# A two-layer hybrid decoder trunk: GpSimd makes the low part of the weights in steps of 128 columns in place of 256

## The reference

```python
for l in range(DEPTH):                                   # DEPTH = 2
    h = rmsnorm(x, norm_g[l]) * (1.0 + scale) + shift    # scale, shift, gate from silu(c) @ w_mod[l]
    parts = split_cols(h @ w_in[l])                      # 1024 x 8224
    y_a = hgrn2_mixer(...) * silu(a_g)                   # 4 heads, gated recurrence
    y_b = mla_mixer(...) * silu(b_g)                     # 8 heads, latent attention
    y_c = retention_mixer(...) * silu(c_g)               # 4 heads
    merged = (sigmoid(m_a) * (y_a @ w_pa[l]) + sigmoid(m_b) * (y_b @ w_pb[l])
              + sigmoid(m_c) * (y_c @ w_pc[l]))
    x = x + gate * (merged @ w_out[l])
return rmsnorm(x, final_g)
```

## Time and profile before

| | before |
|---|---|
| median of 3 runs | 1389.4 us |
| the profiled execution | 1386.04 us |
| its span | 1384.2 us |
| TensorE busy, mean granted clock | 1306.4 us, 94%; 0.986 |
| VectorE busy | 724.0 us, 52% |
| ScalarE busy | 639.5 us, 46% |
| GpSimd busy | 590.7 us, 43% |
| GpSimd, L643, `w_lo` | 736 pieces of 128x256, mean 822 ns, 579.7 us |
| TensorE in the chain of waits | 80% of the span |
| VectorE in the chain of waits | 13% |
| GpSimd in the chain of waits | 0% |

### The profile page before, as it was taken

How to read it: one execution, slowest core, us unless ns; L and a number is a source line. 1 busy time by engine, 2 the same in 40 slices (tenths; PEclk the granted TensorE clock), 3 DMA queues, 4 the chain that set the end, 5 groups by cost and what they waited for, 6 DMA issues and landing times.

```text
span 1384.2 us, 16588 instructions
## 1 busy us (share of the span) xinstructions
PE 1306.4 (94%) x5920; PEld 1036.3 (75%) x5920; DVE 724.0 (52%) x1163; ACT 639.5 (46%) x987; POOL 590.7 (43%) x751
## 2 busy tenths in 40 slices
PE   3999889999999999999979988999999999999996
PEld 2877777787777777788858777778777777778884
DVE  6778786534654434353356777662345431433333
ACT  3365545544554343444335555554355434435431
POOL 3254334654323445455526334445532253454551
PEclk9999999999999999999989999999999999999998
DMA  9322111443222323242212211123312222222221
GB/s 363 121 77 63 60 62 63 142 136 102 77 78 101 126 84 116 98 134 95 94 68 92 77 61 62 65 72 122 107 54 69 77 92 84 91 84 93 98 92 61
DMA packets 40786, 131.84 MB, mean 95 GB/s; under 512 B 5248, under 2 KB 5376, under 8 KB 39424
## 3 DMA queue, kind: packets, MB, share of 16 engines
q1 hardware_dynamic: 30336, 111.57, 23.5%
q10 hardware_dynamic: 10368, 19.21, 4.6%
HBM read 128.13 MB, written 2.10 MB: 94 GB/s over the span
## 4 chain that ended last, share of the span: by engine, by line
PE 80%; DVE 13%; ACT 4%; issue 2%; DMA 1%; POOL 0%; DVEq 0%; ACTq 0%
PE ps_st L760 20%; PE ps_st L762 20%; PE ps_st L761 20%; PE ps_o L782 5%; PE ps_s L811 2%; PE ps_s L856 2%; PE ps_s L880 1%; PE ps_w L865 1%; DVE hg_at L1434 1%; DVE hg_e L1367 1%; PE ps_misc L777 1%; DVE cq_raw L1604 1%; DVE hg_e L1366 1%; PE ps_w L726 1%; PE ps_misc L768 1%
## 5 line engine op out<-in xcount | busy, mean ns | idle before, releaser
L643 POOL TENSOR_TENSOR w_lo<-raw,w_hi 128x256 fp32r<-128x256 f32 x736 | 579.7, 822 | 752.6 <-ACT w_hi L934 752.6
L760 PE MATMUL ps_st<-h_hi,w_hi 128*128 128x512 f32 x984 | 400.3, 407 | 1.0 <-DVE merged L1303 1.0
L762 PE MATMUL ps_st<-h_hi,w_lo 128*128 128x512 f32 x984 | 383.9, 390 | 0.0
L761 PE MATMUL ps_st<-h_lo,w_hi 128*128 128x512 f32 x984 | 383.3, 390 | 0.0
L760 PEld LDWEIGHTS ps_st<-h_hi,w_hi 128*128 128x128 f32 x984 | 184.8, 188 | 45.8 <-issue 7.4
L761 PEld LDWEIGHTS ps_st<-h_lo,w_hi 128*128 128x128 f32 x984 | 185.0, 188 | 42.0 <-issue 6.2
L762 PEld LDWEIGHTS ps_st<-h_hi,w_lo 128*128 128x128 f32 x984 | 184.7, 188 | 39.6
L934 ACT ACTIVATE w_hi<-raw 128x1024 fp32r<-128x1024 f32 x184 | 193.2, 1051 | 26.6 <-PE ps_st L762 23.5
L956 ACT ACTIVATE gate_t<-gate_x 128x512 f32<-128x512 f32 x80 | 50.4, 630 | 230.5 <-DVE gate_x L1252 230.3
L1252 DVE TENSOR_SCALAR gate_x<-ps_st 128x512 f32<-128x512 f32 x79 | 54.4, 689 | 192.0 <-PE ps_st L762 191.8
L958 ACT ACTIVATE gate_t<-gate_t,cs 128x512 f32<-128x512 f32 x80 | 57.9, 724 | 2.6
(11 more groups left out here) (280 smaller groups left out, 2014.5 us busy)
## 6 DMA issues: line engine op xcount, KB each, us to landing
raw<-w_stream SPq DMA_DIRECT2D x184, 512.0 KB, 3.4
mod_w<-w_mod ACTq DMA_DIRECT2D x64, 256.0 KB, 2.7
pro_w<-w_mod_first SPq DMA_DIRECT2D x8, 1024.0 KB, 14.0
x<-x_t SPq DMA_DIRECT2D x4, 512.0 KB, 7.5
ret_decay<-decay ACTq DMA_DIRECT2D x2, 1024.0 KB, 6.3
out_t<-o_t SPq DMA_DIRECT2D x8, 256.0 KB, 2.1
raw_extra<-w_stream SPq DMA_DIRECT2D x2, 512.0 KB, 20.0
cs<-cst SPq DMA_DIRECT2D x1, 836.0 KB, 7.8
```

The lines of the kernel that those rows point to most:

```text
L643: ins = nc.gpsimd.tensor_tensor(lo[:, r], whole[:, r], hi[:, r].bitcast(F32), ALU.subtract)
L760: nc.tensor.matmul(dst[0:m, :], wh, hi, start=(k == 0), stop=False)
L761: nc.tensor.matmul(dst[0:m, :], wh, lo, start=False, stop=False)
L762: last = nc.tensor.matmul(dst[0:m, :], wl, hi, start=False, stop=(k == nk - 1))
```

## The change

GpSimd's loop steps over the columns of an item by `P` = 128 in place of `2 * P` = 256. The data, the arithmetic, and the waits and signals at a burst's ends stay as they are.

```diff
                     pool.wait_ge(w_hi_ready, e.at(w_hi_ready, i + 1))
-                    for a in range(0, n, 2 * P):
-                        r = slice(a, a + 2 * P)
+                    for a in range(0, n, P):
+                        r = slice(a, a + P)
                         ins = nc.gpsimd.tensor_tensor(lo[:, r], whole[:, r], hi[:, r].bitcast(F32), ALU.subtract)
                     ins.then_inc(w_lo_ready, 1)
```

## The result

The changed kernel takes 1370.59 us (median of 4 runs, 1366.31 to 1372.43) against 1388.86 us (median of 4, 1388.32 to 1389.75): 18.3 us faster by the medians. The ratio of the two is given as 0.985, with a 95% interval of 0.983 to 0.988, which is 20.7 us. The forecast was 10.8 us faster, with a range of 1369 to 1389. The direction was right, and the gain was forecast at little more than half of its size.

The account below looks back on a forecast made before the run. The prediction took TensorE as the bound, busy 1306.4 of 1384.2 us. Its terms, -8.0 - 2.0 - 0.8 - 3.0 + 3.0 = -10.8 us, took the median 1389.4 to 1378.6, range 1369 to 1389.

Parts of the forecast that it names:

- Whether the engines disturb each other, and how: GpSimd pieces and VectorE operations reading SBUF take strict turns; each contended operation would wait 0.29 us instead of 0.55.
- term B: TensorE's waits for hg_x: both waits at 84.76 to 88.16 go, three others shorten; -2.0 us, bounds 0 and -3.7.
- The new piece: GpSimd's 128-column piece lasts 0.49 us instead of 0.75, from a slope of 2.02 ns a column.
- Term A: TensorE's waits for hg_kd in the heads: contended VectorE operations ahead wait less; -8.0 us, bounds 0 and -11.
- Term C: TensorE's wait for h_lo at 716.6: three contended operations save 0.26 us each; -0.8 us, bounds 0 and -1.6.
- Term E: Longer GpSimd bursts make low parts late at four places (74.22, 262.48, 730.55, 931.56); +3.0 us, bounds 0 and +11.
- Term D: TensorE's clock falls after four hg_kd waits of 3.73 to 3.76 us; shorter waits save 3 us, bounds 0 and -6.8.
- Rival 1: Another wait stands right behind the shortened one and the clock still falls: -2.8 us, 1386.6 us; chance 0.17.
- Rival 2: VectorE's loss is conserved: twice the pieces, each blocking half as long; only the +3.0 us cost remains, 1392.4; chance 0.10.
- Rival 3: A GpSimd piece is nearly all fixed cost, so new pieces block like old ones: 1408 us; chance 0.03.
- Rival 4: More than forecast: all clock drops go and the hg_kd gain reaches -11: -20 us, 1370 us; chance 0.08.

Follow-up runs that it names:

- e3_fill128: The changed kernel with one extra float32 matmul ahead of TensorE's wait for hg_kd in heads 1 and 2 of each layer: 1364.61 us, 0.982.
- e2_hold256: The kernel before, 256-column pieces, with GpSimd holding back eight bursts a layer until VectorE has passed: 1361.11 us, 0.981.

## Why the prediction was right in direction and too small

**Whether the engines disturb each other, and how:** right for hg_e. It takes strict turns with the pieces, and the loss per turn halves with the piece: 0.27 us where 0.29 was forecast. It is not a rule for all of VectorE: L1413 loses less than a turn, and under term B stands an operation that got no turn for five us.

**The new piece:** 0.467 us against 0.49, a burst of eight undisturbed 3.42 against 3.59. The second size came from an addition in the prologue, and its slope of 2.02 ns was a little low.

**Term A, hg_kd, -8.0: this is the step that failed.** It measured -13.1: 1.55 us in head 0, 1.86 in heads 1 and 2 and 1.28 in head 3, where 0.9, 1.2 and 0.67 stood. hg_e and hg_q were counted nearly rightly (in heads 1 and 2 the four hg_e save 1.17, not 1.04). What the sum had wrong lies behind them. It had hg_qc's two scalings (L1413, L1415) at nothing, without a reason, and gave hg_kd 0.15. The three save 0.27 us each, 0.81 a head, of which L1411's new loss takes back 0.10 to 0.31; the sum had that loss for head 0 only, at 0.29. Heads 1 and 2 thus save 0.69 behind hg_e, where 0.15 stood. Over the eight heads this makes some 4.5 of the missing 5.1 us, and hg_e and hg_q most of the rest. The reason for the slip is visible in the rows above: for the two scalings every instance of before is disturbed, their minimum is 628 and 711 ns, and an even duration looks undisturbed. The shapes should have warned: 128 columns at 0.64 us beside a 256-column subtraction at 0.41.

**Term B, hg_x, -2.0:** -1.0. The two waits at 86 and 88 went, as forecast, but a new one of 0.9 us came at 741.59 in the second layer. Behind it stands a copy on VectorE (L1290), the first row of before, the others of the changed kernel:

```profile
742.50 0.60 DVE L1290 COPY sq_sum<-sq_t 128x512 f32<-128x512 f32 x1 [3.81 <-ACT sq_t L1003]
...
729.75 10.71 POOL L643 TENSOR_TENSOR w_lo<-raw,w_hi 128x128 fp32r<-128x128 f32 x24 [0.73 <-ACT w_hi L934]
735.54 5.20 DVE L1290 COPY sq_sum<-sq_t 128x512 f32<-128x512 f32 x1 [4.70 <-ACT sq_t L1003]
740.77 0.43 DVE L1400 TENSOR_TENSOR hg_x<-hg_e,hg_k 128x256 f32<-128x256 f32 x1
```

Three bursts, 24 pieces, follow each other without a gap, and the copy ends, at 740.74, only after the last of them (740.46). By its record it got no turn in between. In the kernel before three bursts stand in a row there too (738.09 to 748.13), and the copy, in the midst of them, got through in 0.60 us. It lasts 1.81 us in e3_fill128, again with 128-column pieces. What decides whether VectorE gets its turn is open; no run was made for it.

**Term C, h_lo, -0.8:** -0.8.

**Term E, late low parts, +3.0:** +1.8: the waits for w_lo rose from 1.1 to 2.4, and at 76.50, in the first layer's sixth item, 0.46 us of idleness is put down to issue though the burst ended 0.1 before. The first matmuls that answer to the earlier trace rows, and that of the second layer's fourth item:

```profile
76.50 0.47 PE L760 MATMUL ps_st<-h_hi,w_hi 128*128 128x512 f32 x1 [0.46 <-issue]
...
255.29 0.50 PE L760 MATMUL ps_st<-y_hi,w_hi 128*128 128x512 f32 x1 [1.28 <-POOL w_lo L643]
...
729.07 0.50 PE L760 MATMUL ps_st<-h_hi,w_hi 128*128 128x512 f32 x1 [0.70 <-POOL w_lo L643]
...
917.34 0.50 PE L760 MATMUL ps_st<-y_hi,w_hi 128*128 128x512 f32 x1 [0.39 <-POOL w_lo L643]
```

Three of the four places were named; the fourth, at 730.55, was the second layer's third item, which now waits for nothing. At 262 the wait grew by 0.4, not by 1.0. A wait of 1.0 for merged behind it (L1303, at 269), which I had left out of the sum, is gone.

**Term D, the clock, -3:** right for the heads in the profiled execution (two falls of four gone, 3.4 us), but it was only part of what the clock did. TensorE's speed in the first 50 us and between the layers differs from one execution to the next: in the kernel before 24 matmuls stand in the stretch from 44 to 48, in the changed one 13. Its matmuls start 0.4 us earlier at 38 us and 1.7 us later at 66, so 2.1 us are lost between:

```profile
44.00:48.00 4.00, 4.00 (x13) 3.30 (x13) 3.29 (x8) 2.01 (x3) 3.58 (x7) 1.00 0.44 107
```

(The granted clock reads 1.00 there all the same, though matmuls of 0.63 us in place of 0.39 show the lower level.) Between the layers the changed kernel starts its items earlier, and more of them fall into the low clock; that costs 1.5 us, and behind the last sum of squares, at 1359, another 0.6. Together this took back 4.2 us in the profiled execution. Summed over the waits and the clock, -13.1 - 1.0 - 0.8 - 1.0 + 1.8 - 3.4 + 4.2 - 0.4 (the prologue) = -13.7, and the spans differ by 13.7. So in these two executions the sum was off by only 2.9 us, by luck: the 5.1 us that term A lacked were met by 4.2 us of low clock that the sum did not have.

**The profiled executions against the medians.** The times of the two profiled executions differ by 13.6 us, where the medians differ by 18.3: the profiled execution of before lies 2.8 us below its median, that of the changed kernel 1.8 above. The changed kernel's four runs span 6.1 us, and the fastest of them has a granted clock of 0.991 against 0.988. A good part of this spread may be the moment of TensorE's first rise to the full clock, which in the profiled executions of this study lies anywhere from 41 to 51 us; ten us at half speed are worth 5. This is not shown: what sets the moment was not tried, and of the kernels with no fall in the heads e3_fill128 spans 0.2 us but e2_hold256 5.9. So 4.7 us of the 18.3 are in no trace. I had corrected the sum for none of it.

**The rivals.** Rival 1, another wait behind the shortened one, is refuted: the saving at hg_e went through to hg_kd, and TensorE's wait fell by all of it. Rival 2, a conserved loss, is refuted in the heads; for its own case, streams of eight and more contended operations, no run tells. Rival 3 is refuted by the table of sizes. Rival 4 was the nearest; its upper end of A, -11, was still short of -13.1.

## What to carry to other kernels

GpSimd and VectorE, when both read SBUF, mostly take turns instruction by instruction. So GpSimd's instructions are best cut small, or held back, exactly where VectorE is waited for, and left large elsewhere: 64 columns in 17 of the 93 items of a layer gave 28 us, 64 everywhere 9. Smaller pieces also make longer bursts, and turns are not assured: in the changed kernel one copy on VectorE stood behind three bursts for five us. Holding back the few bursts that stand beside the waited-for chain gave the same 28 us by the medians with no smaller pieces at all. Before a group's time is taken as undisturbed, find an instance that is; if there is none, compare it with another shape of its kind.

## What the runs showed of the hardware that I had not expected

- VectorE's scaling of one SBUF tile (L1413, 128 columns) waits for GpSimd's reads too: 0.64 us beside 256-column pieces, 0.29 undisturbed, and 0.29 beside a GpSimd that only writes. Its loss, 0.35 us, is less than the 0.55 of a subtraction of two tiles, and beside 64-column pieces it is nothing.
- The loss of hg_e, a subtraction of two tiles, is 2.0 to 2.2 ns a column over four sizes with no fixed part, though the piece has 0.19 us of it.
- A copy of 128x512 on VectorE (L1290) lasted 5.20 us in the changed kernel, until three GpSimd bursts in a row were over. In the kernel before it lasted 0.60, also amid three bursts in a row.
- A GpSimd multiplication with one input takes longer than the subtraction with two (0.85 against 0.75 us for 256 columns) and costs VectorE 0.20 us in place of 0.55.
- TensorE's clock fell after waits of 1.9 us at two of four places in one execution and at none of four in another kernel's, and a fall of 3.4 us in which TensorE had work cost 1.7 us. Between the layers the low clock lasted 13.6 us in both of the two main executions.
